# Layer 0's last two expert blocks added by one-hot products of TensorE, the other rows by plain loads (2 tiles) and accumulating transfers

## The reference, cut to what matters

```python
def hier_moe(x, ...):                 # 4 groups of 4 experts; top group, top 2 experts of it
...
    h = jnp.einsum('td,edf->tef', t, w_in)
    a, b = jnp.split(h, 2, axis=-1)
    act = jax.nn.silu(a) * b * gates[..., None].astype(h.dtype)
    return jnp.einsum('tef,efd->td', act, w_out).reshape(shp)

xp = layer_norm(ALPHA * xp + hier_moe(xp, ...), ln_g[l, 2], ln_b[l, 2])   # end of a layer
...
cq, ckv, kr = jnp.split(x @ w_in, ...)                                    # start of layer 1
```

## Time and profile before

| | us |
|---|---|
| median of 3 executions | 1103.56 |
| lowest and highest | 1101.9, 1106.04 |
| span of the profiled execution | 1105.1 |
| TensorE busy | 989.1 (90%) |
| VectorE, ScalarE, GpSimd busy | 524.0, 353.4, 253.4 |
| mean granted TensorE clock | 0.927 of full |

### The profile page before, as it was taken

How to read it: one execution, slowest core, us unless ns; L and a number is a source line. 1 busy time by engine, 2 the same in 40 slices (tenths; PEclk the granted TensorE clock), 3 DMA queues, 4 the chain that set the end, 5 groups by cost and what they waited for, 6 DMA issues and landing times.

```text
span 1105.1 us, 17827 instructions
## 1 busy us (share of the span) xinstructions
PE 989.1 (90%) x6978; PEld 617.2 (56%) x6978; DVE 524.0 (47%) x1102; ACT 353.4 (32%) x879; POOL 253.4 (23%) x281
## 2 busy tenths in 40 slices
PE   7998999989989998899998398998999946999994
PEld 6886788887446766533332256657568633333331
DVE  0226520566657657143322654773187571334227
ACT  2335531110011523233432342554115422333423
POOL 2224400051500001536311126300000014362121
PEclk9999999998989987899999698899899956999998
DMA  9434702052205407789997404331434063999976
GB/s 313 91 93 114 232 6 77 5 188 77 67 16 179 192 38 300 271 324 410 404 420 273 176 8 101 79 132 40 136 146 185 31 230 102 337 397 405 418 217 161
DMA packets 81594, 204.17 MB, mean 185 GB/s; under 512 B 22682, under 2 KB 47938, under 8 KB 72288
## 3 DMA queue, kind: packets, MB, share of 16 engines
q1 hardware_dynamic: 60976, 151.83, 37.4%
q0 software_dynamic: 19936, 48.99, 14.4%
q10 hardware_dynamic: 592, 2.13, 0.5%
HBM read 184.92 MB, written 25.92 MB: 191 GB/s over the span
## 4 chain that ended last, share of the span: by engine, by line
PE 75%; DVE 13%; DMA 4%; ACT 4%; issue 3%; POOL 0%; SPq 0%; POOLq 0%; DVEq 0%; ACTq 0%
PE PS L1556 15%; PE PS L1393 10%; PE PS L1035 9%; PE PS L1132 6%; PE PS L1571 6%; PE PS L1416 3%; ACT arena L1923 2%; PE PS L1097 2%; DMA x<-y_tok 2%; PE PS L1023 2%; PE PS L1767 2%; PE PS L1058 2%; PE PS L1777 2%; PE PS L1692 2%; PE PS L1545 2%
## 5 line engine op out<-in xcount | busy, mean ns | idle before, releaser
L1923 ACT ACTIVATE arena<-PS 32x520 f32<-32x520 f32 (+10 forms) x150 | 75.1, 513 | 194.2 <-PE PS L1035 47.3
L1556 PE MATMUL PS<-ring,arena 128*32 128x512 f32 x648 | 116.9, 592 | 1.4 <-DVE arena L2934 1.4
L1556 PE MATMUL PS<-arena 128*32 128x512 f32 x648 | 112.8, 614 | 3.5 <-issue 2.6
L1035 PE MATMUL PS<-xT,ring 128*128 128x260 f32 x448 | 102.2, 389 | 4.1 <-DVE arena L2380 3.1
L1035 PEld LDWEIGHTS PS<-xT,ring 128*128 128x128 f32 x448 | 85.5, 192 | 19.8 <-DVE arena L2380 5.1
L2950 DVE COPY arena<-PS 128x256 f32<-128x256 f32 x24 | 10.2, 424 | 171.2 <-PE PS L1564 171.2
L2194 ACT ACTIVATE arena<-PS,lnc 128x128 f32<-128x128 f32 x192 | 69.5, 473 | 42.8 <-PE PS L1545 42.8
L800 POOL TENSOR_TENSOR rstd<-rstd,small 128x1 f32<-128x1 f32 (+1 forms) x25 | 16.3, 651 | 272.7 <-DVE rstd L2668 245.3
L1571 PE MATMUL PS<-ring,arena 128*32 128x512 f32 x432 | 69.0, 595 | 1.2 <-DVE arena L2950 1.2
L1023 PE MATMUL PS<-ident,x 128*128 128x128 f32 (+1 forms) x240 | 39.4, 319 | 33.0 <-DVE x L2744 20.3
L1132 PE MATMUL PS<-ring,xT 128*128 128x256 f32 (+2 forms) x336 | 66.8, 361 | 0.0
(11 more groups left out here) (422 smaller groups left out, 1858.3 us busy)
## 6 DMA issues: line engine op xcount, KB each, us to landing
arena<-in_moe_w_in_dram SPq DMA_DIRECT2D x27, 1024.0 KB, 10.1
ring<-in_moe_w_in_dram SPq DMA_DIRECT2D x27, 1024.0 KB, 13.5
ring<-in_moe_w_out_dram SPq DMA_DIRECT2D x18, 1024.0 KB, 12.3
ring<-in_w_in_even_dram SPq DMA_DIRECT2D x10, 1024.0 KB, 11.7
xT<-in_moe_w_in_dram SPq DMA_DIRECT2D x10, 1024.0 KB, 13.4
arena<-in_moe_w_out_dram SPq DMA_DIRECT2D x8, 1024.0 KB, 14.5
xT<-in_moe_w_out_dram SPq DMA_DIRECT2D x6, 1024.0 KB, 15.5
y_tok<-in_c_zeros_dram POOLq DMA_DIRECT2D x8, 512.0 KB, 10.2
```

The lines of the kernel that those rows point to most:

```text
L1035: mm = pe.matmul(o[out_rows, 512 * h:512 * h + HALF], lhs(k), rhs(k)[:, HALF * h:HALF * h + HALF], start=(k == 0), stop=(k == nk - 1))
L1556: mm = pe.matmul(o[group(q), 0:512], xT_[:, k, group(q)], w(q, k), start=(k == 0), stop=(k == KD - 1), **quarter(q))
L1923: return act.activation(dst, src, ACT.Copy)
```

## The change

Layer 0 gets the scheme of layer 1, in a mixed form:

- Blocks 10 and 11 of layer 0 are no longer scattered. VectorE builds their one-hot matrices at block 5, and TensorE adds them by `held_blocks` (job cmb, 0, t), 8 records of 128x512 for each of the five tiles (tile 4 has no cheaper form in layer 0).
- The table of layer 0 is also cleared, so GpSimd issues 18 zero transfers instead of nine.
- Tiles 0 and 1: SyncE loads their rows of blocks 0 to 9 (four transfers of 512 KB) at the same place in its order, behind w_uq, and VectorE adds them (p, `loaded_rows`). They wait for ten scatters instead of twelve.
- Tiles 2, 3 and 4: GpSimd adds their rows by six accumulating transfers, issued right behind the tenth scatter.
- VectorE adds the product out of PSUM with the sum over features (c, `held_add`).
- TensorE's order becomes cmb of tiles 0, 1, 2, xT of 0, cmb of 3, xT of 1, oin of 0, cmb of 4, then as before from xT of 2. These eight jobs stand inside a branch (no spilled experts); the code for spilled experts, which now holds a second copy of them, is jumped over behind them.

```diff
-SCATTERED = (BLOCKS_M, BLOCKS_M - 2)
+SCATTERED = BLOCKS_M - 2
+LOADED_TILES = (0, 1)
...
-LATENT_PE = [*LATENT_IN[:-2], ("qn", 0), ("oinT", 3), ("qn", 1), ("oinT", 4)]
+LATENT_HEAD = [("cmb", 0, 0), ("cmb", 0, 1), ("cmb", 0, 2), ("xT", 2, 0), ("cmb", 0, 3), ("xT", 2, 1), ("oin", 0), ("cmb", 0, 4)]
+LATENT_PE = [*LATENT_IN[3:-2], ("qn", 0), ("oinT", 3), ("qn", 1), ("oinT", 4)]
...
-COMBINE_DVE = keys("""a.0 b.0 a.1 s.0 b.1 n.0 a.2 s.1 x.0 r.0 b.2 n.1 a.3 s.2 x.1 r.1 b.3 n.2 a.4 s.3 x.2 r.2 b.4 n.3 s.4 x.3 r.3 n.4 x.4 r.4""")
+COMBINE_DVE = keys("""p.0 p.1 c.0 s.0 c.1 n.0 s.1 x.0 r.0 c.2 n.1 s.2 x.1 r.1 c.3 n.2 s.3 x.2 r.2 c.4 n.3 s.4 x.3 r.3 n.4 x.4 r.4""")
...
-            def expert_rows(l):
+            def expert_rows():
                 for i in range(2):
-                    sp.wait_ge(y_out[i], 16 * BLOCKS_M // 2 * (l + 1))
-                for t in range(NT):
+                    sp.wait_ge(y_out[i], 16 * SCATTERED // 2)
+                for t in LOADED_TILES:
                     for c in range(2):
                         first = c * T + t * P
-                        sp.dma_start(y_of[t][0:ROWS[t], c, :], y_tok[l][first:first + ROWS[t], :]).then_inc(y_in[t][c], 16)
+                        sp.dma_start(y_of[t][:, c, :], y_tok[0][first:first + P, :]).then_inc(y_in[t][c], 16)
...
-                if l == 0:
-                    memory_out(1)
-                else:
-                    pool.wait_ge(s["cleared"], 16 * 9)
+                pool.wait_ge(s["cleared"], 16 * 9 * DEPTH)
...
-                    if b < SCATTERED[l]:
+                    if b < SCATTERED:
                         taken(pool, ("moeY", l, b))
                         rows_out(b % 2, b, y_out[b % 2])
...
+                for i in range(2):
+                    pool.wait_ge(y_out[i], 16 * SCATTERED // 2 * (l + 1))
                 if l:
...
+                else:
+                    for c in range(2):
+                        for t in range(len(LOADED_TILES), NT):
+                            add_rows(t, c)
...
+            for l in range(DEPTH):
+                for first in range(0, 2 * T, P):
+                    n = min(P, 2 * T - first)
+                    load(y_tok[l][first:first + n, :], io["c_zeros"][0:n, :], "cleared")
...
-                if l:
-                    with pe.If(spill_count == 0):
-                        held_blocks()
+                with pe.If(spill_count == 0):
+                    after_blocks()
...
+            def latent_head():
+                steps = {"cmb": lambda l, t: held_blocks(l, [t]), "xT": transpose_x, "oin": oin}
+                for key in LATENT_HEAD:
+                    steps[key[0]](*key[1:])
...
+            def loaded_rows(t):
+                dve.wait_ge(s["x_ready"], t + 1)
+                for c in range(2):
+                    dve.wait_ge(y_in[t][c], 16)
+                    link(dve.tensor_tensor(x[:, t, :], x[:, t, :], y_of[t][:, c, :], ALU.add))
...
+            def held_add(t):
+                r = ROWS[t]
+                total = sums[0:r, t % 3:t % 3 + 1]
+                key = ("cmb", 0, t)
+                if t not in LOADED_TILES:
+                    dve.wait_ge(added[0][t], 32)
+                full(dve, key)
+                free(dve.scalar_tensor_tensor(x[0:r, t, :], pair(key)[0:r, :], 1.0, x[0:r, t, :], ALU.mult, ALU.add, accum_out=total), key)
+                taken(dve, key)
+                mean_of(2, t, total)
```

More of the change, by code:

```diff
@@ L276, in psum_jobs @@
             jobs += [("moe" + s, l, b)] + ([("mkT", 1)] if (l, s, b) == (0, "H", 0) else [])
-    jobs += [("cmb", t) for t in range(NT)]
+    jobs += [("cmb", 1, t) for t in range(NT)]
     return jobs
@@ L509, in decoder_step @@
         slot_gate = part(NB)
-        slot_token = part(NB - SCATTERED[1])
+        slot_token = part(NB - SCATTERED)
         assert at[0] <= ARENA - EXTRA_SLOTS * PIECE
-        y_front = part(3, 2, D, at0=4096)
-        y_of = [y_front[:, t] for t in range(3)] + [pbuf, pT]
+        y_of = [pbuf, pT]
         spill_rows, spill_hot = xs[:, 1, :], xsT[:, 1, :, :].rearrange("p k n -> p (k n)")
@@ L869, in add_rows @@
                     if c:
-                        pool.wait_ge(added[t], 16)
-                    pool.dma_start(x[0:ROWS[t], t, :], y_tok[1][first:first + ROWS[t], :], accum_op=ALU.add).then_inc(added[t], 16)
+                        pool.wait_ge(added[l][t], 16)
+                    pool.dma_start(x[0:ROWS[t], t, :], y_tok[l][first:first + ROWS[t], :], accum_op=ALU.add).then_inc(added[l][t], 16)
+                for i in range(2):
+                    pool.wait_ge(y_out[i], 16 * SCATTERED // 2 * (l + 1))
                 if l:
-                    for i in range(2):
-                        pool.wait_ge(y_out[i], 16 * sum(SCATTERED) // 2)
                     add_rows(0, 0)
@@ L1672, in held_blocks, with oin @@
                     close(mm, key)
+            def oin(t):
+                key = ("oin", t)
+                o = open_(key)
+                taken(pe, ("xT", 2, t))
+                for c in range(2):
+                    landed(pe, ("oin", c))
+                    for k in range(4):
+                        for q, cols in enumerate(LATENT_GROUPS if t == NT - 1 else [slice(0, 416)]):
+                            mm = pe.matmul(o[32 * q:32 * q + ROWS[t], 0:cols.stop - cols.start], xT[:, 4 * c + k, tile_cols(t)],
+                                           wview(("oin", c))[:, k, cols], start=(c == 0 and k == 0), stop=(c == 1 and k == 3), **quarter(q))
+                close(mm, key)
+            def latent_head():
+                steps = {"cmb": lambda l, t: held_blocks(l, [t]), "xT": transpose_x, "oin": oin}
+                for key in LATENT_HEAD:
+                    steps[key[0]](*key[1:])
             def latent_attention():
@@ L1681, in oin_back @@
                         mm = pe.transpose(o[:, c * P:c * P + r], src, ident[0:r, 0:r])
[L1682 to L1693, removed]
                     close(mm, key)
@@ L2230, in experts @@
                 with spilled(act, l):
[L2231 to L2234, removed]
+                    per = PER_SPILL[0]
                     for j in range(SPILL):
@@ L2976, in experts @@
                     steps_s = [0]
-                    per = PER_SPILL[l][0]
+                    per = PER_SPILL[0]
                     full(dve, ("moeY", l, BLOCKS_M - 1))
-                    if l:
-                        for t in range(NT):
-                            dve.wait_ge(added[t], 32)
+                    for t in range(NT):
+                        if l or t not in LOADED_TILES:
+                            dve.wait_ge(added[l][t], 32)
+                        else:
+                            dve.wait_ge(s["x_ready"], t + 1)
                     for j in range(SPILL):
```

117 lines of the change are left out of this document (48 added, 69 removed).

## The result

The changed kernel takes **1113.89 us** (median of 4 runs, 1109.78 to 1116.34) against 1103.62 us for the kernel before (4 runs, 1101.9 to 1106.04): ratio 1.0095, 95% interval [1.007, 1.0119]. It is slower by more than the 0.5% that can be told here. The forecast was 1111.5 us, slower.

The account below looks back on a forecast made before the run. TensorE, busy 90% of the span, bounds the kernel; tile 2's turning was the yardstick. Tile 0's turning at 625.3, plus 14.6 work, 1.85 clock and 1.3 jump, gave 643.0, 8.1 us later: 1111.5 us, range 1100 to 1115.5.

Parts of the forecast that it names:

- TensorE's side: Behind the experts' last product: five one-hot products take 17.5 us, three of them (10.5 us) in the hole before tile 0's turning.
- Bound of 4.6 us for the gain: At tile 2's turning: 630.3 against 634.94 if VectorE keeps up; no arrangement of this order can be earlier.
- The loads: DMA from 597: weights, plain loads and adds take 20.6 us; last load lands at 618.6, tile 0's sum starts at 619.8.
- Turns packet by packet: At the DMA engines from 597: packets of q0 (adds) and q1 (loads) are taken in turn, so q0 drains first.
- Adding packets at twice the price: At the DMA engines: an adding packet costs twice a plain one; six adding transfers take 10.8 us.
- From the sum to the turning of tile 0: From the start of tile 0's add with the sum to its turning (mean, squares, power, norm): 5.5 us.
- The clock: After TensorE's pause before tile 0's turning: slow clock until about 629 adds 1.85 us (none to 3.5).
- The jump: Behind tile 4's one-hot product: skipping the spilled experts' code waits for instruction fetch, 1.3 us taken, between 0 and 2.6.
- The sum: Tile 2's turning: 625.3 + 14.6 + 1.85 + 1.3 = 643.0 against 634.94, 8.1 us later.
- At nothing: Edits costed at zero: nine more zero transfers, one-hot operations at block 5, GpSimd's six issues (over by some 609), new waits.
- The signs named: Around 605 to 620: three products behind 605, VectorE idle until 614, TensorE waiting 8 to 10 us, clock 0.50, both queues full.
- the cover works: Rival at the last plain load: it lands before 608.9, TensorE's work becomes the bound, 1099 to 1101 us; chance 0.2.

Follow-up runs that it names:

- e1: The changed kernel without layer 0's six adding transfers (rows of blocks 0 to 9 left out for tiles 2, 3 and 4): 1100.43 us, ratio 0.9959 to the kernel before.
- e2: The changed kernel with GpSimd's adding transfers waiting until the last plain load has landed: 1105.47 us, ratio 1.0007 to the kernel before.
- e10: The changed kernel with 13 added products 128x512 in TensorE's pause ahead of tile 0's turning: 1111.43 us, ratio 1.0067 to the kernel before.
- e9: The changed kernel as it is, measured again: 1110.75 us, ratio 1.006 to the kernel before.
- e7: e3 with tile 4's one-hot product in four quarters of 256 columns, as in layer 1: 1102.9 us, ratio 0.9979 to the kernel before.
- e4: The kernel before with layer 0's table also cleared and waited for (18 zero transfers instead of 9): 1105.52 us, ratio 1.0004 to the kernel before.
- e5: e3 with GpSimd's adding transfers issued only when the last plain load has landed: 1104.03 us, ratio 0.9983 to the kernel before.
- e3: The changed kernel with the four plain loads issued ahead of the second w_in_odd piece and w_uq: 1100.47 us, ratio 0.9958 to the kernel before.
- e11: e3 as it is, measured a second time: 1098.7 us, ratio 0.9955 to the kernel before.
- e8: The changed kernel with 11 added products 128x512 in TensorE's pause ahead of tile 0's turning: 1110.8 us, ratio 1.0051 to the kernel before.

## Why the prediction was right

The mechanism held: the one-hot products did not cover the wait, because the plain loads landed behind the adds.

- **TensorE's side.** Three products in 10.5 us: 10.6. Bound of 4.6 us for the gain: e1 reached 4.4.
- **The loads.** The last load was forecast for 618.6 and landed at 619.1; the sum of tile 0 was forecast for 619.8 and started at 620.50. The wait that ended last was not quite the forecast's: VectorE was released by the second load, at 616.6, and the three adds that it still had to do (3.9 us) ended just behind the last load and its one add. The two paths differ by 0.2 us here. Adding up the 20.6 us of DMA work from 597 on was right, and that gaps in q0 do not help held, as q1 did end last: q0 moved its last packet at 616.4. Turns packet by packet: 249 against 275 from 608 to 615. The Trainium skill (DMA: Bandwidth & Descriptors, section Queues, rings and completion order) states turns between the queues by packet, with 9 to 17 descriptors as typical of a packet. The near equal counts agree with turns; whether the profile's packets of some 4 KB are the page's packets no run here tells.
- **Adding packets at twice the price**: 0.31 against 0.15 us. e1 and e2 show that the adds beside the loads made them late.
- **From the sum to the turning of tile 0**: 5.5 predicted, 5.07 measured. The power in it took 0.57 us, where POOL's one instruction in that stretch before had 1.48. Of these 0.9 us only 0.4 are seen, since tile 1's sum stands ahead of tile 0's last step in VectorE's order and ended at 624.6.
- **The clock.** 1.85 us predicted, between 0 and 3.5; 2.3 by the comparison with e10 (1.2 in e9). It was back at 2.4 GHz at about 631, not at 629.
- **The jump was the term mis-sized.** I took 1.3 us of 0 to 2.6. In the changed kernel it cost 0: no pause stands behind tile 4's product. e7 shows what the cover is worth: 2.50 us of pause when it is thinner. That this is near the upper bound of 2.6 us is luck, as the bound was made of two fetches and the pause has one in it. The right question was not how much the jump costs but how long the work is that the sequencer has already handed on. The Trainium skill (Runtime: NRT & Kernel Launch, section Instruction fetch mechanics) says that a taken branch to code outside the fetched window waits for a fetch. The pause of 2.50 us in e7 with its one fetch agrees; in the changed kernel such a wait does not show, as work in hand covers it.
- **The sum.** 643.0 predicted, 642.67 measured: +0.7 for the loads, -0.4 for the norm, +0.4 for the clock, -1.3 for the jump, and +0.2 for the work between the turnings. The errors nearly cancelled, which is luck; none was above 1.3 us. The stretch came out 7.7 us longer, and 6.8 in e9, against 8.1 forecast, and the two medians of the changed kernel, 1113.89 and 1110.75, lie on both sides of 1111.5. The kernel before's profiled execution was farther from its median than was said: all other executions took 1.6 to 2.1 us more than their spans, so the one with the span of 1105.1 took about 1107, an estimate, over 3 us above the median. The forecast adds the 8.1 us to the median and is not touched by it.
- **At nothing**: the zeros (e4). In the changed kernel the ring piece issued beside them landed 26.5 us after 124.55, thus at 151, and is first used at about 186. GpSimd's issues: over by 609.2, as said; e2 and e5 show how near this is to a wait.
- **The signs named.** The three products directly behind 605, VectorE's wait until 613, q1 ending last and the clock of 0.50 came. TensorE's wait was 10.18 us, just over the 8 to 10. The wait of 1 us before tile 2's turning did not come.
- **The rival "the cover works"** is not wrong as a mechanism: e3 nearly reaches it, with a pause of 0.56 us, by the order of four DMAs. What I overlooked is that the prediction's own list of DMA work has the weights first, and nothing needs them first: w_uq is first used 50 us later. The order of the loads on SyncE was a part of the change that I costed as given.

## What to carry to other kernels

When products cover a wait for DMA, work out what the DMA engines must carry before the cover ends, in the order in which the queues serve it: here reordering four loads ahead of weights that were not yet due turned 0.6 to 1% slower into 0.4% faster. An accumulating transfer is no spare capacity beside a critical load: here it took about a turn for each of the load's packets, at twice the time. Before moving a waiting DMA issue on an engine that computes too, look for the small instruction behind it.

## What the runs showed of the hardware

- GpSimd's queue began late in three runs, all with the loads ahead of the weights: in e3, e11 and e7 q0 moved its first packet 4.5 to 4.6 us behind the first add's issue (at 595.46, 594.77 and 596.52), while q1 had 95 to 99% of the engines. In the changed kernel, with q1 at 69%, it was 1.7 us (issue at 594.93), and in e2, with the engines free, 1.7 us too. Full engines alone are not the whole cause: in e5, with q1 at 94%, it was 2.4 us. What the cause is was not tried. e3 and e11 owe part of their gain to it.
- TensorE's clock fell to 1.2 GHz behind pauses as short as 2.23 us (e8) and 2.50 us (e7); 0.56 us (e3) left it at 2.4 GHz. In e8 the fall came 1.4 us after work had begun again, so tile 0's turning (1.12 us) was still at 2.4 GHz and tile 3's product (5.30 us) was not.
